# A layer's first tiles, the end of its FFN and the final output rearranged in a hybrid decoder kernel

## The reference

```
h    = rmsnorm(x) * g;  proj = h @ w_in          # 32 tiles of 128 columns, and 8 columns for dt
mix  = [RG-LRU | retention | Mamba-2 SSD](proj)  # convolutions, scans, chunked attention
x    = x + mix @ w_out
h    = rmsnorm(x) * g;  gate, up = h @ w_up      # D_FF = 2816 each
x    = x + (gelu(conv3(gate)) * up) @ w_down
y    = rmsnorm(x)                                # once, at the end
```

## Time and profile before

| | us |
|---|---|
| median of three runs | 3016.21 |
| profiled execution | 3004.08 |
| its span, first to last instruction | 3002.3 |
| PE busy | 2843.9 (95%) |
| DVE busy | 1636.3 (55%) |
| POOL busy | 1020.6 (34%) |
| ACT busy | 582.9 (19%) |

### The profile page before, as it was taken

The page is one execution under the profiler, slowest core; times in us unless marked ns, Lnnn a source line. Parts: engine busy times, 40 slices in busy tenths (PEclk is TensorE's granted clock), DMA queues, the critical chain, the costliest instruction groups (busy, mean ns, idle before and its releaser), DMA issues.

```text
span 3002.3 us, 46964 instructions
## 1 busy us (share of the span) xinstructions
PE 2843.9 (95%) x18164; PEld 2779.3 (93%) x18164; DVE 1636.3 (55%) x2122; ACT 582.9 (19%) x887; POOL 1020.6 (34%) x444
## 2 busy tenths in 40 slices
...
GB/s 151 117 72 138 104 124 147 72 113 45 43 49 43 48 49 42 49 49 42 53 93 90 99 127 93 121 150 142 37 43 44 49 44 48 49 43 48 49 42 76
DMA packets 75817, 227.94 MB, mean 76 GB/s; under 512 B 18672, under 2 KB 19696, under 8 KB 74624
## 3 DMA queue, kind: packets, MB, share of 16 engines
q1 hardware_dynamic: 75680, 226.12, 22.6%
...
## 4 chain that ended last, share of the span: by engine, by line
PE 85%; DVE 6%; issue 4%; DMA 2%; SPq 1%; POOL 1%; PEld 1%; ACT 0%; DVEq 0%; POOLq 0%; ACTq 0%; PEldq 0%
PE ps L670 26%; PE ps L672 25%; PE ps L671 25%; DVE sb_pt L1349 1%; DMA sb_ch<-sin 1%; PE ps L780 1%; SPq L457 1%; PE ps L803 1%; PE ps L838 1%; PE ps L782 1%; PE ps L901 1%; PE ps L815 0%; PE ps L814 0%; PE ps L785 0%; PE ps L902 0%
## 5 line engine op out<-in xcount | busy, mean ns | idle before, releaser
L670 PE MATMUL ps<-sb_h_hi,sb_w_hi 128*128 128x344 f32 x3744 | 1221.1, 326 | 40.3 <-POOL sb_w_lo L652 34.0
L671 PE MATMUL ps<-sb_h_lo,sb_w_hi 128*128 128x344 f32 x3744 | 1203.5, 321 | 0.0
L672 PE MATMUL ps<-sb_h_hi,sb_w_lo 128*128 128x344 f32 x3744 | 1202.6, 321 | 0.0
L649 POOL TENSOR_TENSOR sb_w_hi<-sb_w_raw,sb_ones 128x1024 fp32r<-128x1024 f32 x220 | 427.0, 1941 | 1906.2 <-PEq L1011 878.2
L670 PEld LDWEIGHTS ps<-sb_h_hi,sb_w_hi 128*128 128x128 f32 x3744 | 712.0, 190 | 50.8 <-issue 45.4
L671 PEld LDWEIGHTS ps<-sb_h_lo,sb_w_hi 128*128 128x128 f32 x3744 | 711.8, 190 | 1.4
L672 PEld LDWEIGHTS ps<-sb_h_hi,sb_w_lo 128*128 128x128 f32 x3744 | 711.2, 190 | 0.0
L652 POOL TENSOR_TENSOR sb_w_lo<-sb_w_raw,sb_w_hi 128x1024 fp32r<-128x1024 f32 x220 | 593.5, 2698 | 17.3
L670 PE MATMUL ps<-sb_y_hi,sb_w_hi 128*128 128x344 f32 x1536 | 506.8, 330 | 41.3 <-DVE sb_x L1339 19.2
L672 PE MATMUL ps<-sb_y_hi,sb_w_lo 128*128 128x344 f32 x1536 | 498.0, 324 | 0.0
L671 PE MATMUL ps<-sb_y_lo,sb_w_hi 128*128 128x344 f32 x1536 | 495.0, 322 | 0.0
...
## 6 DMA issues: line engine op xcount, KB each, us to landing
...
```

Source lines behind the costliest of these rows:

```text
L649: nc.gpsimd.tensor_tensor(w_hi[:, q, :], w_raw[:, q, :], ones[:, 0:1].to_broadcast([P, 1024]), ALU.mult).then_inc(sg.sem("w_hi_done"), 1)
L670: mm(o, wh, ah, start=first, stop=False)
L671: mm(o, wh, al, start=False, stop=False)
L672: return mm(o, wl, ah, start=False, stop=last)
```

## The change

It has six parts.

1. *Start of a layer.* PE begins with four k-steps of tile 24 alone (slot 0), then waits for slot 1 and does the same four of tile 25, then k-steps 4 to 7 of both.
2. *First tiles.* ACT copies tiles 25 and 24 from PSUM to ev as they are, as soon as each is complete; DVE multiplies them in place by rstd later, 24 first. PE runs the first third of tile 26 ahead of spread_rstd and the second third ahead of turning dt. SP handles tile 24 first.
3. *FFN, last block.* The loop runs nine times; the up slots of block 10 follow it in the open. Then: one down slot of block 9 (output tiles 0 to 3), one of block 10 (the same tiles), and two slots that hold rows of blocks 9 and 10 together (512 rows, four k-steps) for output tiles 4 and 5, and 6 and 7. The split y of block 10 lies in h_hi and h_lo, k-steps 6 and 7, which refresh must therefore leave alone until PE is through.
4. *DVE in that part.* After the products of block 10: two additions, then y_lo, then two more, and in the last stretch eight additions with refresh.
5. *Last norm.* PE waits for the last sum of squares and not for the last h_lo.
6. *Output.* Eight places (two of ev, six of pt) instead of two.

The diff in its core, in the order: counts and tiles, SP, PE at a layer's start, PE at the end of the FFN, ACT, DVE at a layer's start.

```diff
-RUSES = 12 * FB
+LOOPED = FB - 2
+END = 12 * LOOPED
+RUSES = END + 20
+    def out_tile(m):
+        return ev[:, m, :] if m < 2 else pt[:, m - 2, :]
+    def Yf(last):
+        return (h_hi[:, KD - 2:KD, :], h_lo[:, KD - 2:KD, :]) if last else (y_hi[:], y_lo[:])
...
-                    sp.wait_ge(*sg.after("t0_free"))
+                    sp.wait_ge(*sg.after("t0_scaled"))
-            main(FIRST[1])
             main(FIRST[0])
+            main(FIRST[1])
-            sp.dma_start(io["y"][m], ev[:, m % 2, :]).then_inc(*sg.on(f"y_stored{m % 2}", m, 16))
+            sp.dma_start(io["y"][m], out_tile(m)).then_inc(*sg.on(f"y_stored{m % 2}", m, 16))
...
+            slot_ready(0)
+            pe.wait_ge(sg.sem("m_free"), layer * RUSES + (M0 - 1))
+            for k in range(4):
+                pe.wait_ge(sg.sem("h_split"), layer * (2 * KD) + (k + 1))
+                tile_k(4, 0, k, False)
             slot_ready(1)
             pe.wait_ge(sg.sem("m_free"), layer * RUSES + M0)
-            for k in range(KD):
+            for k in range(4):
+                tile_k(0, 1, k, False)
+            for k in range(4, KD):
                 pe.wait_ge(sg.sem("h_split"), layer * (2 * KD) + (k + 1))
...
-            pe.wait_ge(*sg.after("dt_taken"))
-            spread_rstd("mix")
             pe.wait_ge(*sg.after("t1_free"))
             run([("in", 26, 0)])
+            pe.wait_ge(*sg.after("dt_taken"))
             pe.wait_ge(*sg.after("t0_free"))
+            spread_rstd("mix")
+            run([("in", 26, 1)])
+            pe.wait_ge(*sg.after("rstd_ready", "mix"))
...
-            run([("in", 26, 1), ("in", 26, 2)])
+            run([("in", 26, 2)])
...
+            for j in range(4):
+                ffn_slot("up", j % 2, END + 4 + j, 0, SLOTS - 8 + j)
+            pe.wait_ge(sg.sem("ffn_split"), layer * FB + (FB - 1))
+            ffn_slot("down", 0, END + 8, 0, SLOTS - 4)
             pe.wait_ge(sg.sem("ffn_split"), layer * FB + FB)
+            ffn_slot("down_last", 1, END + 12, 0, SLOTS - 3)
             for j in range(2):
-                ffn_slot("down", j, 4 + 4 * j, 12 * (FB - 1), 48 + j, 6 * (FB - 1))
+                ffn_slot("both", j, END + 16 + 2 * j, 0, SLOTS - 2 + j)
...
-        pe.wait_ge(sg.sem("h_split"), (2 * DEPTH + 1) * KD)
+        pe.wait_ge(*sg.after("sq_used", ("next", KD - 1)))
...
+            act.wait_ge(sg.sem("h_split"), layer * (2 * KD) + KD)
+            act.wait_ge(*sg.after("t1_ready"))
+            af(g3(ev[:, 1, :]), ps[:, 0:3, 0:TG], ACT.Identity).then_inc(*sg.on("t1_free"))
+            act.wait_ge(*sg.after("t0_ready"))
+            af(g3(ev[:, 0, :]), ps[:, 4:7, 0:TG], ACT.Identity).then_inc(*sg.on("t0_free"))
...
+            if key == "next" and m == KD - 2:
+                act.wait_ge(sg.sem("m_ready"), layer * RUSES + RUSES)
...
-            v.tensor_tensor(g3(ev[:, 1, :]), ps[:, 0:3, 0:TG], g3(rstd[:]), ALU.mult).then_inc(*sg.on("t1_free"))
-            v.tensor_tensor(g3(ev[:, 0, :]), ps[:, 4:7, 0:TG], g3(rstd[:]), ALU.mult).then_inc(*sg.on("t0_free"))
+            v.tensor_tensor(ev[:, 0, :], ev[:, 0, :], rstd[:], ALU.mult).then_inc(*sg.on("t0_scaled"))
+            v.tensor_tensor(ev[:, 1, :], ev[:, 1, :], rstd[:], ALU.mult).then_inc(*sg.on("t1_scaled"))
```

More of the change, by code:

```diff
@@ L616, in _ @@
                                      raw[:, j, SEQ:T + 2]).then_inc(*sg.on(f"ffn_stored{j}", "loop", 16))
-            for s in (SLOTS, SLOTS + 1):
-                weights(s)
+            for s in range(8):
+                weights(SLOTS - 6 + s)
+                if s in (1, 3):
+                    j = s // 2
+                    sp.wait_ge(*freed(layer, END + 4 + j))
+                    step()
+                    sp.dma_start(io["o_ffn_new"][layer, 2 * FB - 2 + j],
+                                 raw[:, j, SEQ:T + 2]).then_inc(*sg.on(f"ffn_stored{j}", "end", 16))
             for j in range(2):
@@ L997, in ffn_slot @@
                 pe.wait_ge(sg.sem("w_split_done"), layer * SLOTS + slot_base + (s + 1 + FREE))
-                n = KD if kind == "up" else 2
-                a, b_ = (h_hi, h_lo) if kind == "up" else (y_hi, y_lo)
-                for i in range(1 if kind == "up" else 4):
+                n, pieces = {"up": (KD, 1), "down": (2, 4), "down_last": (2, 4), "both": (4, 2)}[kind]
+                for i in range(pieces):
                     r = r0 + i
@@ L1258, in ffn_block @@
             def ffn_block(blk, tag, base):
+                yh, _ = Yf(tag == "end")
                 for j in range(2):
@@ L1280, in _ @@
             ffn_block(0, "first", 0)
-            with act.Fori(0, FB - 1) as b, sg.loop("ffn", FB - 1, b):
+            with act.Fori(0, LOOPED) as b, sg.loop("ffn", LOOPED, b):
                 ffn_block(b + 1, "loop", b * 12 + 4)
+            ffn_block(FB - 1, "end", END + 4)
             for m in range(KD):
-                act.wait_ge(*freed(layer, 4 + m, 12 * (FB - 1)))
+                act.wait_ge(*freed(layer, END + 12 + m))
                 refresh(m, layer * 2 + 2, "next")
@@ L1802, in y_part, with y_rest, down @@
                                     ALU.mult).then_inc(*sg.on("ffn_y", (tag, j)))
+            def y_rest(tag):
+                yh, yl = Yf(tag == "end")
                 for j in range(2):
                     dve.wait_ge(*sg.after("ffn_hi", (tag, j)))
-                    ins = v.tensor_tensor(y_lo[:, j, :], pt[:, 2 + j, :], y_hi[:, j, :].bitcast(F32), ALU.subtract)
+                    ins = v.tensor_tensor(yl[:, j, :], pt[:, 2 + j, :], yh[:, j, :].bitcast(F32), ALU.subtract)
                 ins.then_inc(*sg.on("ffn_split", tag))
+            def down(mo, r, base, tag):
+                dve.wait_ge(sg.sem("m_ready"), layer * RUSES + base + (r + 1))
+                v.tensor_tensor(g3(x[:, mo, :]), ffn_bank(r)[:, :, 0:TG], g3(x[:, mo, :]),
+                                ALU.add).then_inc(*sg.on("m_free", (tag, r)))
@@ L1819, in _ @@
-            dve.wait_ge(*sg.after("ffn_split", "loop"))
+                    down(mo, 8 + mo, b * 12, "ffn")
+                y_product("loop", 7, b * 12)
+                y_rest("loop")
+            up_part(FB - 1, "end", END + 4, 0)
+            y_product("end", END + 7, 0)
+            for mo in range(2):
+                down(mo, END + 8 + mo, 0, "end")
+            y_rest("end")
+            for mo in range(2, 4):
+                down(mo, END + 8 + mo, 0, "end")
+            dve.wait_ge(*sg.after("ffn_split", "end"))
```

64 lines of the change are left out of this document (33 added, 31 removed).

## The result

The changed kernel takes 2983.04 us (median of six runs, 2975.85 to 2993.1), the one before 3009.85 (six runs in the same series; the 3016.21 that the forecast counted from was the median of three). The ratio is 0.991, 95% interval 0.9890 to 0.9929, so 21 to 33 us are gone. The forecast was 2985. The profiled execution took 2983.0 with a span of 2981.2, 21.1 less than the span before, where the sum of the prediction had 30.7. The median agrees and the profiled pair does not quite, so the steps have to be read one by one.

What follows compares the result with a forecast made beforehand. PE was taken as the bound (85% of what ended last). 3004.1 - 16.9 - 10.4 + 1.5 - 0.6 - 4.3 = 2973.4 us profiled; against the median, 3016.2 - 30.7 = 2985.5, stated as 2985, range 2970 to 3000.

Steps and rivals of the forecast that it cites:

- FFN's last block: Down pieces: DVE's two products take 5.39 us beside POOL's split, PE waits 2.2, and the 6.2 us y_lo wait goes.
- PE now does four k-steps of tile 24 meanwhile. A wait of 0.8 is left: Next layer's start: 5.65 us of PE work covers most of POOL's 6.4 us split of slot 1, leaving 0.8 us.
- if the wait for slot 1 stays near 6 us: Between the layers: a listed sign that the prediction is wrong; it expected under 1.5 us for slot 1.
- The second layer's end: Last up slot to token sums: 52.3 us instead of 62.7, 10.4 less, with the clock staying low.
- Output: Program's end: with eight places the tiles go 1.3 us apart without waiting for a store; 4.3 us less.
- Clock after the new waits: After the new 2.2 us wait, twice in the program, the clock may fall: 0 to 3.4 us, 1.5 more taken.
- The layer's start: Tiles 26 and 27: 5.4 us won, mostly lost to slot 3's later load; 0.3 us less per layer, 0.6 in all.
- R2: Rival: slot 3's load lands 2 us later, PE idles 5.6 us per layer; gain about 25, 2992 us; chance 0.13.
- R4: Rival: the weight stream's lag continues past slot 3, PE idles 3.6 us at slot after slot; 3029 us; chance 0.03.
- the boundary: Last up slot of the first layer to the next token sums: 70.95 us against 87.9, 16.9 less.

Runs made afterwards that it cites:

- run 8: Kernel after with DVE's order in FFN's last block changed to product, addition, product, addition; ratio 0.9883 to the kernel before, 2976.05 us.
- run 4: Kernel after with FFN's end and the last norm's wait as before the change, the other parts kept; ratio 0.9989 to the kernel before, 3002.76 us.
- run 3: Kernel after with PE's layer loop written out twice, so PE does not jump between the layers; ratio 0.9867 to the kernel before, 2967.25 us.
- run 10: Kernel after with the edits of run 3, run 7 and run 8, plus 30 filler matmuls at each layer's end; ratio 0.9835 to the kernel before, 2964.67 us.
- run 6: Kernel after with the output through two buffers again, all else kept; ratio 0.9930 to the kernel before, 2990.80 us.
- run 7: Kernel after with loads of slots 3 and 4 issued ahead of the store of tile 24; ratio 0.9869 to the kernel before, 2974.23 us.

## Why the prediction was right, and where not

*FFN's last block: right.* Two products under POOL's split 5.28 (5.39 taken), a wait of 2.12 (2.2), y_lo in time, no lag of DVE later, 49.1 with 1.6 of low clock. The rule on the shared port in the Trainium skill, page "SBUF — State Buffer", section "SBUF: two separate sides", agrees with run 8: the product with two SBUF inputs is held until w_lo has ended (2.30 us, where one takes half of 2.37 alone), the addition with one input in PSUM is not (1.22).

*"PE now does four k-steps of tile 24 meanwhile. A wait of 0.8 is left": this step failed.* The sum had no term for the jump. In every run with the loop and the new order 4.0 to 5.6 us went by behind PE's jump back to the top of the layer, nearly the whole time of the split, and then came a restart at the low clock (25.0 for the 144 matmuls, not 22.6). From the end of the down pieces to the token sums I had 23.45 us and it was 30.7 by the windows. By the prediction's own list it was wrong here: "if the wait for slot 1 stays near 6 us", and PE's idle time is 5.56; and the way from the last up slot to the token sums is 79.8, not 71. The 6.78 us of the kernel before hid this: there the jump lay under the real wait for slot 1 (in run 4, with the same end of FFN, it is 4.18), and I took the releaser that the profile named for the whole reason. The step's own arithmetic was sound: without the jump it is 22.98 (run 3), and worth 7.4 in the trace.

*The second layer's end: right*, 10.3 for 10.4, and the clock was at 0.50, as said. What a clock that stays up would give I had priced at some 4 us; the end of run 10 shows 3.3.

*Output: 4.3 forecast*, 5.0 in the two traces, 4.3 in run 6.

*Clock after the new waits: 1.5 forecast for both.* Of the sixteen such waits of 2.1 us in the profiled runs with the old order of products, four were followed by the low clock, 1.5 us each. So 0.8 per execution on average, inside the bounds.

*The layer's start: right in its pieces*, load of 5.0 us (slot 3's split starts at 61.57; landing at 61.9 was forecast), wait of 3.10 (3.6), low clock behind it, 0.9 left at split 5 for 0.3. R2 and R4 didn't occur: the new waits for w_lo are those of slot 3, 3.10 and 2.62, and the two of 5.9 later in the layers stand in the kernel before too. But what a start gains was the wrong question, since even the 4.7 us of run 7 shrink to about 1 in the first layer.

*Why the total was right all the same.* In the profiled pair the boundary fell short by 8.8 of its 16.9 (7.2 in the failed step, 1.6 in the low clock, for which 1.5 stood apart in the sum, so 7.3 net), the second layer's end by 0.1, the 0.6 of the layers' starts were not left at T, and the second layer's middle took 2.4 longer; the output gave 0.7 more. That makes 9.7, against the 9.6 between 30.7 and 21.1. The medians show 26.8 (21 to 33), nearer to the forecast, and the difference of some 5 us between a single pair and the medians is within the spread above. A right total here is partly luck, twice: one term was 7 too large, and the measured gain is at the upper side of what the places add up to; and the gain was subtracted from 3016.2, where six runs give 3009.85. A gain 3.9 too large and a base 6.4 too high leave the forecast within 2 us of the time.

What stays open: why run 3 gains 13 to 16 where the boundary shows 7, and run 7 9 to 12 where its trace shows 4. By the ratios both are within the sum of the two intervals, and more executions, not other kernels, would be needed.
